# One-core hybrid block on Trainium2: gate products, weights and exponentials of the selective attention in another order, one projection panel loaded earlier

## What is computed

```python
o_cmp = softmax(q kc^T - slope * dist)  vc        # 31 compressed blocks
o_slc = softmax over the selected key blocks      # 8 blocks of 64 keys: all causal ones at 512 tokens
o_win = softmax over the last 256 keys
o_ns  = gates[..., 0:1] * o_cmp + gates[..., 1:2] * o_slc + gates[..., 2:3] * o_win
mix   = sigmoid(gate_dn) * (o_dn @ w_proj_dn) + sigmoid(gate_nsa) * (o_ns @ w_proj_nsa)
x     = x + mix @ w_out
```

## Time and profile before

| | us |
|---|---|
| median of three runs | 2688.28 |
| profiled execution, its own time | 2686.47 |
| its span | 2684.7 |
| PE busy (share of the span) | 2533.4 (94%) |
| DVE busy | 1144.0 (43%) |
| ACT busy | 973.7 (36%) |
| POOL busy | 1322.5 (49%) |

### The profile page before, as it was taken

One profiled execution on the slowest core, in us unless ns is written; L12 is line 12 of the kernel. 1 busy time (PEld: TensorE's weight loads), 2 busy tenths in 40 slices (PEclk: granted clock), 3 DMA queues, 4 the chain that ended last, 5 costly groups with the idle time before them and its releaser, 6 DMA issues.

```text
span 2684.7 us, 42605 instructions
## 1 busy us (share of the span) xinstructions
PE 2533.4 (94%) x16743; PEld 2157.1 (80%) x16743; DVE 1144.0 (43%) x2061; ACT 973.7 (36%) x1723; POOL 1322.5 (49%) x754
## 2 busy tenths in 40 slices
PE   8988999999997999999899899999999989999999
PEld 7967999999994888878678688888766667788887
DVE  6874422124697432112567645201778802320210
ACT  4344422223445342222455422433565542321221
POOL 4762766567675276656844411222211165564552
PEclk9988999999999899999999899999999999899999
DMA  5210222322321022232323100222111142222322
GB/s 162 79 48 17 79 94 71 102 88 72 107 64 47 17 94 90 82 109 76 96 63 115 43 2 2 84 73 63 56 48 48 48 165 94 79 94 94 94 95 78
DMA packets 175661, 203.70 MB, mean 76 GB/s; under 512 B 6436, under 2 KB 160647, under 8 KB 175255
## 3 DMA queue, kind: packets, MB, share of 16 engines
q1 hardware_dynamic: 172176, 199.57, 23.0%
q10 hardware_dynamic: 3334, 2.06, 0.3%
HBM read 193.23 MB, written 8.39 MB: 75 GB/s over the span
## 4 chain that ended last, share of the span: by engine, by line
PE 77%; DVE 6%; ACT 4%; POOL 4%; issue 3%; POOLq 2%; DVEq 1%; DMA 1%; ACTq 1%; SPq 0%
PE ps L744 18%; PE ps L745 17%; PE ps L746 17%; PE ps L1610 7%; PE ps L993 4%; POOL wlo L2948 3%; POOLq L2993 2%; PE ps L1487 1%; ACT p_slc L2105 1%; PE ps L1432 1%; ACTq L2107 1%; PE ps L1246 1%; ACT p_t L2162 1%; PE ps L1467 1%; POOL conv L2991 1%
## 5 line engine op out<-in xcount | busy, mean ns | idle before, releaser
L2948 POOL TENSOR_TENSOR wlo<-wraw,whi 128x1024 fp32r<-128x1024 f32 x364 | 877.8, 2433 | 858.0 <-ACT whi L1694 857.8
L744 PE MATMUL ps<-hn_hi,whi 128*128 128x264 f32 (+1 forms) x2400 | 825.2, 344 | 19.2 <-POOL wlo L2948 8.1
L745 PE MATMUL ps<-hn_lo,whi 128*128 128x264 f32 (+1 forms) x2400 | 816.5, 340 | 0.0
L746 PE MATMUL ps<-hn_hi,wlo 128*128 128x264 f32 (+1 forms) x2400 | 813.6, 339 | 0.0
L1694 ACT CAST whi<-wraw 128x2048 fp32r<-128x2048 f32 x182 | 346.5, 1904 | 536.8 <-PE ps L746 361.1
L744 PEld LDWEIGHTS ps<-hn_hi,whi 128*128 128x128 f32 x2400 | 454.5, 189 | 74.7 <-issue 11.5
L746 PEld LDWEIGHTS ps<-hn_hi,wlo 128*128 128x128 f32 x2400 | 454.5, 189 | 51.1
L745 PEld LDWEIGHTS ps<-hn_lo,whi 128*128 128x128 f32 x2400 | 455.0, 190 | 47.4
L744 PE MATMUL ps<-ff_hi,whi 128*128 128x264 f32 (+1 forms) x528 | 170.2, 322 | 6.6 <-POOL wlo L2948 6.6
L745 PE MATMUL ps<-ff_lo,whi 128*128 128x264 f32 (+1 forms) x528 | 169.6, 321 | 0.0
L746 PE MATMUL ps<-ff_hi,wlo 128*128 128x264 f32 (+1 forms) x528 | 169.4, 321 | 0.0
(11 more groups left out here) (478 smaller groups left out, 4198.3 us busy)
## 6 DMA issues: line engine op xcount, KB each, us to landing
wraw<-in_w_in SPq DMA_DIRECT2D x54, 1024.0 KB, 5.2
wraw<-in_w_gate_up SPq DMA_DIRECT2D x44, 1024.0 KB, 5.1
wraw<-in_w_up SPq DMA_DIRECT2D x16, 1024.0 KB, 5.5
wraw<-in_w_down SPq DMA_DIRECT2D x16, 1024.0 KB, 5.0
wraw<-in_w_out SPq DMA_DIRECT2D x12, 1024.0 KB, 5.0
wraw<-in_w_down SPq DMA_DIRECT2D x16, 768.0 KB, 4.3
wraw<-in_w_down SPq DMA_DIRECT2D x16, 640.0 KB, 4.1
gate_dram<-gate_out SPq DMA_DIRECT2D x16, 256.0 KB, 2.2
```

The costliest lines, as they stand in the source:

```text
L744: nc.tensor.matmul(dst, whi[:, slot, c:c + P], rhs_hi, start=start, stop=False)
L745: nc.tensor.matmul(dst, whi[:, slot, c:c + P], rhs_lo, start=False, stop=False)
L746: return nc.tensor.matmul(dst, wlo[:, slot, c:c + P], rhs_hi, start=False, stop=stop)
L2948: last = nc.gpsimd.tensor_tensor(wlo[:, slot, part], wraw[:, slot, part], whi[:, slot, part].bitcast(F32), ALU.subtract)
```

## The change

PE's gate chunks are spread: one after the first two turns of the selected blocks, one after the selected products, one after the first two turns of the window blocks, one ahead of the compressed product, four at the end (before: three, and five at the end). `window_scores(u + 1)` moves ahead of the last selected product, and the compressed turn moves among the window products.

GpSimd weighs heads 2 and 3 of the selected probabilities, DVE heads 0 and 1. DVE makes the factor of the next unit inside `window_in` and weighs its two heads at the end of it. `gate_copy(u)` moves from the next iteration of DVE's loop, where it stood after the window and compressed weights, to the end of its own. On GpSimd the panel splits of the stage stand between these weights.

ACT's selected exponentials are split in two and two around the first two window copies. In the last unit `dn_upper(range(0, 4))` stands after these.

SP issues panel `PN_MDN + 2` before it waits for the gate stores, and panel 3 between the loads of `merged` and `sig2`; the sigmoids of `merged` wait for its own load alone.

```diff
-            for done in gate_stored:
-                sp.wait_ge(done, 16 * UNITS // 2)
+            panel(N0 + PN_MDN + 2, 0, cols_of("w_proj_dn_2", PW * 2))
+            for moved in gates_moved:
+                sp.wait_ge(moved, 16 * UNITS // 2)
             sp.wait_ge(o_taken, UNITS)
-            sp.dma_start(merged, ...).then_inc(sig_in, 16)
-            sp.dma_start(sig2, ...).then_inc(sig_in, 16)
+            sp.dma_start(merged, ...).then_inc(gates_moved[0], 16)
+            panel(N0 + PN_MDN + 3, 1, cols_of("w_proj_dn_2", PW * 3))
+            sp.dma_start(sig2, ...).then_inc(gates_moved[1], 16)
             sp.dma_start(x2, x2_dram).then_inc(x2_moved, 16)
-            for j in range(2, 4):
-                panel(N0 + PN_MDN + j, j % 2, cols_of("w_proj_dn_2", PW * j))
...
+            def selected_out(u):
+                n = units[u][1] + 1
+                pe.wait_ge(weigh_step, 4 * u + 2)
+                pe.wait_ge(slc_weighed, u + 1)
+                for b in range(min(n, 2)):
+                    block_turned(u, "slc", p_slc[u % 2], b)
+                gate_fill(u, range(0, 1))
+                for b in range(n):
+                    if b == n - 1 and u + 1 < UNITS:
+                        window_scores(u + 1)
+                    block_out(u, "slc", vs, b, b)
+                    if b + 2 < n:
+                        block_turned(u, "slc", p_slc[u % 2], b + 2)
+            def window_out(u):
+                g, t = units[u]
+                n, first = min(t + 1, 3), first_key(t) // P
+                def next_turned(b):
+                    if b < n:
+                        block_turned(u, "win", p_win[u % 2], b)
+                    elif b == n:
+                        pe.wait_ge(weigh_step, 4 * u + 4)
+                        turn(("cmp", u, 0), [p_cmp[u % 2].rearrange(flat)])
+                pe.wait_ge(weigh_step, 4 * u + 3)
+                next_turned(0)
+                next_turned(1)
+                gate_fill(u, range(2, 3))
                 for b in range(n):
+                    block_out(u, "win", vw, b, first + b)
+                    next_turned(b + 2)
+                gate_fill(u, range(3, 4))
...
-                pe.wait_ge(p_weighed, 3 * u + 1)
-                key_blocks_out(u, "slc", p_slc[u % 2], vs, 0)
-                if u + 1 < UNITS:
-                    window_scores(u + 1)
-                gate_fill(u, range(0, 3))
-                pe.wait_ge(p_weighed, 3 * u + 2)
-                key_blocks_out(u, "win", p_win[u % 2], vw, first_key(units[u][1]) // P)
-                compressed_out(u)
-                gate_fill(u, range(3, KD))
+                selected_out(u)
+                gate_fill(u, range(1, 2))
+                window_out(u)
+                gate_fill(u, range(4, KD))
...
                 block_copies(u, "slc", t + 1)
                 if u + 1 < UNITS:
-                    exponentials(u + 1, 0)
-                if u == UNITS - 1:
+                    exponentials(u + 1, 0, range(0, 2))
+                window_copies(u, range(0, 2))
+                if u + 1 < UNITS:
+                    exponentials(u + 1, 0, range(2, REP))
+                else:
                     dn_upper(range(0, 4))
-                block_copies(u, "win", min(t + 1, 3))
-                turned_copy(("cmp", u, 0), pc_t, lambda bank: ps[:, bank, 0:P])
+                window_copies(u, range(2, 4))
...
                 scaled_top(u, B_WIN).then_inc(tops_ready, 1)
+                weigh(u, B_SLC)
...
                 dve.wait_ge(exps_done, 3 * u + step)
+                if branch == B_SLC and u:
+                    dve.wait_ge(slc_weighed, u)
...
+                last = nc.vector.tensor_tensor(factor, factor, own[:, branch, :], ALU.mult)
+                if branch == B_SLC:
+                    last.then_inc(weigh_step, 1)
+                    return
...
             for u in range(UNITS):
                 weigh(u, B_WIN)
                 weigh(u, B_CMP)
-                if u:
-                    gate_copy(u - 1)
                 if u + 1 < UNITS:
                     selected_in(u + 1)
                     window_in(u + 1)
-                    weigh(u + 1, B_SLC)
-            gate_copy(UNITS - 1)
+                    weighed_heads(p_slc[(u + 1) % 2], P * (units[u + 1][1] + 1), B_SLC, 2)
+                gate_copy(u)
...
-            for pn in range(PN_Z, PN_GATE + 7):
+            def weigh_selected(u):
+                p, w = p_slc[u % 2], P * (units[u][1] + 1)
+                pool.wait_ge(weigh_step, 4 * u + 1)
+                for r in range(2, REP):
+                    last = nc.gpsimd.tensor_scalar(p[:, r, 0:w], p[:, r, 0:w], s_weight[:, B_SLC, r:r + 1], None, ALU.mult)
+                last.then_inc(slc_weighed, 1)
+            for pn in range(PN_Z, PN_GATE):
                 lower(N0 + pn + 2, pn % 2)
+            for u in range(UNITS):
+                weigh_selected(u)
+                if u >= 3 and u % 2:
+                    pn = PN_GATE + (u - 3) // 2
+                    lower(N0 + pn + 2, pn % 2)
```

More of the change, by code:

```diff
@@ L1493, in compressed_out, with block_turned, block_out @@
-            def compressed_out(u):
-                g, _ = units[u]
-                pe.wait_ge(p_weighed, 3 * u + 3)
-                turn(("cmp", u, 0), [p_cmp[u % 2].rearrange(flat)])
+            def block_turned(u, kind, p, b):
+                turn((kind, u, b), [p[:, r, P * b:P * (b + 1)] for r in HEAD_ORDER])
+            def block_out(u, kind, v, b, block):
+                g, _ = units[u]
+                k = turn_no[kind, u, b]
+                pe.wait_ge(p_t_ready, k + 1)
+                if kind == "slc" and b == 0 and u:
+                    pe.wait_ge(o_taken, u)
+                for i in range(2):
+                    last = nc.tensor.matmul(out_sums()[HD * i:HD * (i + 1), :], v[:, block, HD * g:HD * (g + 1)],
+                                            p_t[:, k % 2, 2 * P * i:2 * P * (i + 1)],
+                                            start=(kind == "slc" and b == 0), stop=False, skip_group_check=True)
+                last.then_inc(pv2_done, 1)
@@ L2094, in head_rms, with exponentials @@
                 nc.scalar.activation(n_rms[:, a:b], ps[:, 6, a:b], ACT.Sqrt, bias=eps6, scale=1.0 / HD)
-            def exponentials(u, part):
+            def exponentials(u, part, heads=range(REP)):
                 slot, (_, t) = u % 2, units[u]
-                act.wait_ge(tops_ready, 3 * u + part + 1)
+                if heads[0] == 0:
+                    act.wait_ge(tops_ready, 3 * u + part + 1)
                 if part == 2:
@@ L2166, in block_copies, with window_copies @@
                     turned_copy((kind, u, b), p_t[:, turn_no[kind, u, b] % 2, :], lambda bank: ps[:, bank, :])
+            def window_copies(u, blocks):
+                n = min(units[u][1] + 1, 3)
+                for b in blocks:
+                    if b < n:
+                        turned_copy(("win", u, b), p_t[:, turn_no["win", u, b] % 2, :], lambda bank: ps[:, bank, :])
+                    elif b == n:
+                        turned_copy(("cmp", u, 0), pc_t, lambda bank: ps[:, bank, 0:P])
             def out_copy(u):
@@ L2857, in weigh, with weighed_heads @@
                     p = p_cmp[slot][:, :, 0:N_CMP]
-                    nc.vector.tensor_tensor(p, p, wide(factor, [P, REP, N_CMP], 2), ALU.mult).then_inc(p_weighed, 1)
+                    nc.vector.tensor_tensor(p, p, wide(factor, [P, REP, N_CMP], 2), ALU.mult).then_inc(weigh_step, 1)
                     return
-                p, w = (p_slc[slot], P * (t + 1)) if branch == B_SLC else (p_win[slot], P * min(t + 1, 3))
-                for r in range(REP):
+                weighed_heads(p_win[slot], P * min(t + 1, 3), branch, REP)
+            def weighed_heads(p, w, branch, heads):
+                for r in range(heads):
                     last = nc.vector.tensor_scalar(p[:, r, 0:w], p[:, r, 0:w], s_weight[:, branch, r:r + 1], None, ALU.mult)
-                last.then_inc(p_weighed, 1)
+                last.then_inc(weigh_step, 1)
             def gate_copy(f):
@@ L2872, in _ @@
             window_in(0)
-            weigh(0, B_SLC)
+            weighed_heads(p_slc[0], P * (units[0][1] + 1), B_SLC, 2)
             for u in range(UNITS):
```

41 lines of the change are left out of this document (12 added, 29 removed).

## The result

The changed kernel is slower: 2729.47 us median of 4 runs (2716.45 to 2730.35) against 2693.29 of the kernel before on the same chip, ratio 1.0114 with an interval of 1.0082 to 1.0146, so 30.7 us more (22 to 39). The forecast was 5.6 less. The profiled execution took 2730.35 us (span 2728.6).

The account below looks back on a forecast made before the run. PE was taken to bound the stage, with DVE close behind. Stage +5.9 and merge -11.5 gave -5.6 us: the profiled 2686.47 would become 2680.9, the median 2682.7, with a range of 2662 to 2704.

Parts of the forecast that it names:

- Two blocks of 2.35 put selected_in at 8.0, window_scores at 8.4 where PE wanted it at 4.8: Unit 11, likewise 3 and 7: the panel split blocks DVE's weights twice, +1.4 us a unit in place of -2.5.
- I take one, +2.1: Units 5, 9, 13: the split blocks one short two-input instruction of the compressed weights, +2.1 us each; bounds -0.1 and +4.6.
- Unit 0 has no gate copy ahead: -2: Unit 0, DVE's queue: no copy of gates stands ahead of its weights, so the unit gets 2 us shorter.
- second rival: Two blocks in units 5, 9, 13: +7 us, 2690; chance 0.20 together with the case of none there.
- against it that the two instructions last 0.5 us together: Units 5, 9, 13: argument against two blocks, that the two short compressed-weight instructions last only 0.5 us together.
- VectorE's late start behind the copy: Every unit with a gate copy ahead: selected_in starts 3.2 to 3.5 us after the opening, 1.3 to 2.1 later than before.
- the gates' cover of ACT's copies: Stage: gate chunks between turn and copy hide ACT's 0.6 us copies; PE's 14.6 us of waits for them shrink.
- the merge to a few tenths: Merge: the early panel removes PE's 10.3 us stop and 2.0 of slower products, leaving a 0.8 stall: -11.5 us.
- had been made before P: Units 9 to 11 before the change: window and compressed weights were finished before the unit's opening; selected_in began 1.4 to 2.2 us after it.
- third rival: POOL's heads close a loop, as DVE cannot weigh while POOL holds the port: +26 us, 2709; chance 0.14.
- if POOL's pair of heads is over 2 us: Sign that the forecast is wrong; it had taken 1.2 us for a pair at 512 columns, 0.6 at 256.
- first rival: Splits slip clear of DVE's weights, or DVE gets through between the halves: 19.2 us faster still, 2663.5; chance 0.24.

Follow-up runs that it names:

- warm: Changed kernel with the first gate chunk's three products issued five times more in six units, ahead of the window scores: 2712.63 us, ratio 1.0059.
- the mended order: Changed kernel with gate copy back, splits behind the compressed weights, unit 0's heads early: 2675.92 us, ratio 0.9907; with all four heads on VectorE 2670.05 us, 0.9906.

## Why the prediction was wrong, step by step

By units 0 to 13 (opening of 0 to opening of 14), in us; "warm" is the run with more work:

| units | before | forecast | changed | warm |
|---|---|---|---|---|
| 0 | 13.3 | 11.2 | 20.1 | 20.1 |
| 4, 8, 12 | 39.8 | 38.9 | 43.2 | 40.0 |
| 1 | 15.3 | 15.2 | 15.3 | 15.3 |
| 5, 9, 13 | 45.8 | 52.1 | 65.5 | 58.3 |
| 2, 6, 10 | 56.7 | 55.5 | 56.1 | 56.1 |
| 3, 7, 11 | 52.2 | 56.4 | 63.6 | 59.1 |
| sum | 223.0 | 229.2 | 263.7 | 248.8 |

The 34.5 us between forecast and result fall into these steps.
- **The clock, 14.9** (changed less warm). The steps "Two blocks of 2.35 put selected_in at 8.0, window_scores at 8.4 where PE wanted it at 4.8" and "I take one, +2.1" priced a stall of PE at its length. The row at the lower clock was read, and used for the merge alone. After 4.1 us of standing the next 9 us went at 0.50 (0.57 in the stretch where it rose again), and unit 7's 2.7 us had the same behind it:

```profile
2056.00:2059.00 3.00, 2.42 (x20) 2.03 (x20) 2.83 (x11) 0.64 (x3) 0.00 (x0) 0.70 0.00 0
2059.00:2062.00 3.00, 3.00 (x13) 2.17 (x10) 2.06 (x9) 0.45 (x3) 0.00 (x0) 0.50 0.00 0
2062.00:2065.00 3.00, 3.00 (x15) 1.87 (x13) 0.50 (x3) 2.10 (x6) 0.05 (x1) 0.66 0.01 3
```

- **Unit 0, 8.9.** The term "Unit 0 has no gate copy ahead: -2" followed VectorE's queue and not GpSimd's. The step that was added there, two heads, stood behind a split that waits for ACT. The run that moved it took all 8.9 off unit 0: 6.7 of waiting, and 2.2 of slower products behind it.
- **One block or two in units 5, 9, 13, 6.2** (58.3 less 52.1). The second rival's "against it that the two instructions last 0.5 us together" was the error: blocked, they last as long as the halves do. The trace decided for two in all of them, the second rival's number; unit 9's rows show both short instructions blocked (2.12 and 2.34), and so do those of all three units in the run with more work. In units 5 and 13 of the changed kernel the split started up to 1 us earlier than forecast, and one of its blocks (unit 5) or both (unit 13) fell on window weights. By the rule of the Trainium skill, SBUF — State Buffer, section "Who interferes with whom", that I had set beside this step, both short instructions would be blocked: unit 9 agrees with it.
- **Units 3, 7, 11, 2.7; the rest, 1.8.** Two blocks as forecast; up to 0.8 a unit of warm's 19.7 may be its added products, which outlast the 2.7 us stall there.

What held: VectorE's late start behind the copy (units 1, 2, 8 and 10 within 0.6 us), the place and number of blocks in units 3, 7, 11, the gates' cover of ACT's copies, the merge to a few tenths. The second rival had the right blocks and still came to 2690, since it too left out the clock and unit 0. Two slips of the working are small beside this: two blocks in three units are +7.5 by its own bounds, not +7, and "had been made before P" does not fit unit 11 of the earlier trace rows, whose weights end 1.5 us behind P.

The third rival had the sign but not the mechanism. A pair of heads takes 1.9 us at 256 columns and 2.7 at 384, over the 1.0 from which it was to decide, and the sign "if POOL's pair of heads is over 2 us" was met; yet without them the stage stays. It assumed that VectorE can't weigh while GpSimd does. In unit 8 GpSimd's pair runs from 2082.05 to 2083.91 and VectorE's two heads from 2082.59 for 1.01 us, inside it. The first rival was 24.8 us under the kernel before. With the splits waiting and unit 0 mended, so that no block is left, the kernel is 10.5 us under it (ratio 0.9961), with the copy back in its place and unit 0 mended 14 (0.9948). Only all three edits together give its number (0.9907), and with one block left in units 3, 7 and 11. So its number needed more than free weights: the late copy costs of itself.

What each part of the change is worth, by the runs:

- The early panels: -11.6 in the merge.
- The copy's place and the splits' start depend on each other. The stage with unit 0's heads early, in us:

| | splits as in the change | splits held back |
|---|---|---|
| copy late, as in the change | 291.7 | 258.8 |
| copy at its old place | 260.3 | 246.0 |

The copy's place costs 31.4 where the splits are free to meet the weights and 12.8 where they are not; the splits' start costs 32.9 with the copy late and 14.3 with it back. In the changed kernel about 15 us of this is the lower clock.

- All the rest (chunks between turns, split exponentials, window scores one product earlier, the factor inside `window_in`): the stage is 260.3 with the splits where the change has them and 246.0 with them held back, against 258.2 before. What does not hang on the splits shows in units 0, 4, 8 and 12, which take 11.2 us in both and 13.3 before, 8.3 together. The kernel before with its splits held back was not run, nor were the chunks and the exponentials tried apart from each other, so what each brings stays open.
- Two heads on GpSimd: nothing in the mended order, and 6.5 in the changed one by unit 0.

## What to carry to other kernels

When a wait is put at the head of a queue, work out what now runs under the other engine's long instructions, and count one full block for each of the long instructions, on whatever short one it meets, not the short ones' summed length. Price a stall of TensorE of some microseconds with the slower products behind it as well: here 15 us behind 25 us of waiting. Before calling a later mend a gain of the first change, run the old kernel with the same mend. And follow the first pass of a loop separately, on every queue: what stands ahead of the loop is not what stands ahead inside it.

## What the runs showed of the hardware

- TensorE's granted clock was at 0.50 after stands of 2.7 us (unit 7) to 4.1 us (unit 9), for some 7 and 10 us (the last microsecond of unit 9's stand among them). How long it stayed low did not follow the length of the stand: after 4.4 us in unit 13 it was low for some 3 us. Stands of 1.5 us in units 4 and 12 had some 3 us of it behind them in the changed kernel, and unit 4's had none with the splits held back. The stand of 1.8 us in unit 8 had none in the changed kernel and some 7 us of it with the splits held back, where the unit took 16.5 us in place of 13.6. Products in the gap, 15 of 0.23 us, held the stage at 0.99 and made the kernel faster by more than they cost.
- GpSimd's tensor_scalar in place costs 0.61, 0.94, 1.37 and 1.71 us at 128, 256, 384 and 512 columns. At 512 columns that is above the 0.61 of its copy and the 1.2 of its two-input split, the two rows between which I had placed it. By the Trainium skill, GPSIMD Engine Reference, section "Engine selection", one input runs at roughly line rate; this form does not: VectorE takes 0.40 to 0.42 us for the 384 columns that cost GpSimd 1.37.
- One long two-input instruction of GpSimd blocked VectorE for its whole length and its successor blocked the next one; GpSimd's one-input tensor_scalar did not, though it slowed VectorE: two heads of 256 columns took 1.01 us beside it, where four took 1.14 with GpSimd idle. Nor did it block a two-input instruction: VectorE's 128x124 product of the compressed probabilities (L2868), 0.29 us with GpSimd idle, took 0.44 us inside the same pair and at most 0.66 inside the others. Reductions, reciprocals and reads of PSUM ran under the split at their usual price (0.27, 0.18 and 0.60 to 0.69 us).
